# A norm gain folded into the weights' high/low split, a new order of the first tiles, and a shorter output norm in a hybrid block

## The reference

```python
hn = rms_norm(x, attn_norm)                  # x * rsqrt(mean(x^2) + eps) * gain
proj = hn @ w_in                             # one combined projection
qkv = silu(causal_depthwise_conv(proj[qkv columns], conv_w))
q = l2_normalize(q) * 128 ** -0.5            # 4 heads of 128; k likewise without the factor
o_a = gated_delta_rule(q, k, v, g, beta)     # chunks of 64 tokens, state carried over
o_a = rms_norm(o_a, gdn_out_norm) * silu(gate)
o_b = multiscale_pool(proj[pool columns]);  o_c = chunk-causal attention (MLA)
x = x + concat(o_a, o_b, o_c) @ w_out
x = x + SwiGLU(rms_norm(x, ffn_norm)) @ w_down
```

## Time and profile before

| | |
|---|---|
| Median of 3 runs | 1188.63 us (1188.12 to 1191.61) |
| The profiled execution | 1188.19 us, of which the span from first to last instruction is 1186.2 us |
| Instructions in the span | 16437 |
| Input projection, tiles 2 to 21 | 41 to 301 us |
| Delta rule and attention | about 300 to 475 us |
| Output projection and SwiGLU | from about 500 us to the end |

### The profile page before, as it was taken

The page is one execution under the profiler, slowest core; times in us unless marked ns, Lnnn a source line. Parts: engine busy times, 40 slices in busy tenths (PEclk is TensorE's granted clock), DMA queues, the critical chain, the costliest instruction groups (busy, mean ns, idle before and its releaser), DMA issues.

```text
span 1186.2 us, 16437 instructions
## 1 busy us (share of the span) xinstructions
PE 1176.0 (99%) x6049; PEld 974.6 (82%) x6049; DVE 812.8 (69%) x1246; ACT 445.4 (38%) x778; POOL 386.1 (33%) x351
## 2 busy tenths in 40 slices
PE   8999999999999999999999999999999999999998
PEld 7888878887788888888888888888888888888887
DVE  6548777997778764447765665656565687868686
ACT  5322222432333332345433333333333353535342
POOL 5001111440221221024456565665665346000000
PEclk9999999999999999999999999999999999999999
DMA  8411344683575210424246656554684369565544
GB/s 265 128 36 36 107 123 119 192 243 103 145 247 148 72 58 1 160 89 125 85 153 216 203 178 220 180 169 151 213 302 141 115 205 317 175 200 173 168 144 172
DMA packets 196980, 186.14 MB, mean 157 GB/s; under 512 B 23495, under 2 KB 152917, under 8 KB 196901
## 3 DMA queue, kind: packets, MB, share of 16 engines
q1 hardware_dynamic: 196750, 185.05, 49.7%
q10 hardware_dynamic: 150, 0.05, 0.0%
HBM read 126.75 MB, written 57.26 MB: 155 GB/s over the span
## 4 chain that ended last, share of the span: by engine, by line
PE 53%; ACT 0%; DVE 0%; issue 0%
PE ps L2629 35%; PE ps L2634 18%; ACT hT L1551 0%; PE ps L2566 0%; DVE x L2162 0%
## 5 line engine op out<-in xcount | busy, mean ns | idle before, releaser
L2629 PE MATMUL ps<-xop,wop_hi 128*128 128x512 f32 x1232 | 379.5, 389 | 0.0
L2629 PEld LDWEIGHTS ps<-xop,wop_hi 128*128 128x128 f32 x1232 | 231.0, 188 | 48.4 <-DVE wop_lo L2074 0.6
L2629 PE MATMUL ps<-xop,wop_lo 128*128 128x512 f32 x616 | 239.6, 389 | 0.0
L2634 PE MATMUL ps<-dop,wop_hi 128*128 128x512 f32 x440 | 136.0, 390 | 0.1
L2629 PEld LDWEIGHTS ps<-xop,wop_lo 128*128 128x128 f32 x616 | 115.6, 188 | 24.1
L2074 DVE TENSOR_TENSOR wop_lo<-w_sumS,wop_hi 128x512 fp32r<-128x512 f32 (+1 forms) x104 | 83.1, 802 | 67.1 <-ACT wop_hi L1521 67.1
L2074 DVE TENSOR_TENSOR wop_lo<-w_pair,wop_hi 128x512 fp32r<-128x512 f32 (+1 forms) x76 | 84.7, 1115 | 34.1 <-ACT wop_hi L1521 34.1
L2162 DVE TENSOR_TENSOR x<-x,ps 128x512 f32<-128x512 f32 x112 | 76.6, 684 | 45.5 <-PE ps L2634 45.2
L2213 PE MATMUL ps<-act_hi,w_hi 128*128 128x512 f32 x320 | 100.7, 396 | 0.2 <-DVE stage L1787 0.2
L2213 PE MATMUL ps<-act_lo,w_hi 128*128 128x512 f32 x320 | 98.8, 390 | 0.0
L2213 PE MATMUL ps<-act_hi,w_lo 128*128 128x512 f32 x320 | 98.6, 389 | 0.0
(11 more groups left out here) (364 smaller groups left out, 2157.3 us busy)
## 6 DMA issues: line engine op xcount, KB each, us to landing
w_pair<-in_w_gate_up SPq DMA_DIRECT2D x44, 512.0 KB, 5.3
hidden<-up SPq DMA_DIRECT2D x22, 512.0 KB, 2.9
wd_rows<-in_w_down SPq DMA_DIRECT2D x22, 512.0 KB, 5.2
raw<-in_w_in SPq DMA_DIRECT2D x21, 512.0 KB, 4.6
wd_raw<-down_sums SPq DMA_DIRECT2D x12, 768.0 KB, 7.1
down_sums<-wd_rows SPq DMA_DIRECT2D x33, 256.0 KB, 2.6
wd_raw<-in_w_down SPq DMA_DIRECT2D x9, 768.0 KB, 8.0
qkv_kept<-qkv_st SPq DMA_DIRECT2D x12, 512.0 KB, 5.4
```

What stands on the lines that cost most here:

```text
L2629: last = pe.matmul(ps[:, bank, :].rearrange("p (t n) -> p t n", n=P), w[:, k, :], a[:, k, :, :], start=(p in ("P1", "P2", "P7") and k == 0 ...
L2634: last = pe.matmul(ps[:, bank, :], w[:, k, :], a[:, k, :], start=(p in ("P1", "P2", "P7") and k == 0 and w is wop_hi[s] and a is hi), stop ...
```

## The change

It does five things.

- The gain attn_norm is no longer multiplied into the tokens. It comes in as 8 rows of 128, PE turns it into a column per block (in_gain), and the tokens are multiplied by rstd alone, by a tensor_scalar.
- The gain goes into the weights at the split. As it differs from block to block, split_hi and split_lo become 8 instructions over 128 columns each in place of one over 1024; each has in_gain[:, k] as its factor per partition. This holds for every tile from 1 to 21; the narrow tile is multiplied once.
- At the start: 14 and 8 warm-up matmuls in place of 5 and 4, no spreading of the gain row, token tile 3 turned before the narrow tile, the quarter of tile 1 after more of the narrow tile; ACT squares a token tile after act_hi of the one three before, not ahead of it; the splits of tiles 0 and 1 come one step later on ACT, and one and two steps later on DVE. SP's order of loads is the same as before, though the loop is written in another way.
- The output norm of the delta rule goes under one root: mean(o^2) * rq^2 + eps becomes mean(o^2) + 128 * eps * (ss + eps), whose inverse root is the whole factor. The root of the queries' square sums on POOL and four small DVE instructions in each chunk go.
- The first inverse step reads A's lower left 32x32 blocks directly (32 rows in place of 64) and no longer a masked copy B. POOL's m0 stage, its mask, and the wait on it go.

Left out of the diff: the constants and the mask tensor, and POOL_ORDER without its qk and m0 entries.

```diff
--- before.py
+++ after.py
@@ -282,9 +280,10 @@
...
     x_sq = prep[:, 0, :]
-    x_gain_row = prep[:, 2, :]
+    gain_rows = prep[0:KT, 2, 0:P]
     x_in = [sgT[:, j, :] for j in range(3)] + [prep[:, 1, :]] + [cT[:, j, :] for j in range(2)] + [x_six[:, :], pz[:, 0, :]]
-    C_CONV, C_FFN, C_QA, C_KVA, C_GDN, C_POOL, C_POS, C_QK = 0, 48, 56, 58, 59, 60, 62, 70
+    C_CONV, C_FFN, C_QA, C_KVA, C_GDN, C_POOL, C_POS, C_QK, C_IN = 0, 48, 56, 58, 59, 60, 62, 70, 72
+    in_gain = cols[:, C_IN:C_IN + KT]
 
...
@@ -352,9 +351,9 @@
...
 
-        mid_pe = Steps(sem("mid_pe"), ["gain0", "gain1", "cols", "decays", "log_row", "pool0", "pool1"])
+        mid_pe = Steps(sem("mid_pe"), ["in_gain", "cols", "decays", "log_row", "pool0", "pool1"])
         mid_act = Steps(sem("mid_act"), ["exp_abs", "exp_alog", "exp_b", "ln", "kr_sq", "kv_weights", "decays", "log_col", "log_row", "pool0", "pool1"])
-        mid_dve = Steps(sem("mid_dve"), ["positions", "abs", "kv_scaled", "one_plus", "g"])
+        mid_dve = Steps(sem("mid_dve"), ["in_gain", "small_scaled", "positions", "abs", "kv_scaled", "one_plus", "g"])
 
...
@@ -388,10 +387,10 @@
...
         ga = [Steps(sem(f"gdn_act{b}"), ["sq", "x1", "m1", "x2", "osq"], ahead=True) for b in range(2)]
-        gd = [Steps(sem(f"gdn_dve{b}"), ["et", "att", "ss", "kd", "vn", "rqs", "r2", "n1", "n2", "r0", "r", "o1",
-                                         "v", "s", "o", "osum", "oms0", "oms", "of", "on", "out"], ahead=True)
+        gd = [Steps(sem(f"gdn_dve{b}"), ["et", "att", "ss", "kd", "vn", "n1", "n2", "r0", "r", "o1",
+                                         "v", "s", "o", "osum", "oms", "on", "out"], ahead=True)
               for b in range(2)]
-        gg = [Steps(sem(f"gdn_pool{b}"), ["rq", "b0", "sd", "pow"], ahead=True) for b in range(2)]
+        gg = [Steps(sem(f"gdn_pool{b}"), ["sd", "pow"], ahead=True) for b in range(2)]
         GROUPS = (1, 0)
...
@@ -765,7 +764,8 @@
...
             load_in_tile(1, 1)
-            for t in range(RAW, TT):
+            load_x(RAW)
+            for t in range(RAW + 1, TT):
                 load_x(t)
...
@@ -1177,16 +1167,7 @@
...
                 for stage_name, b, i in order:
-                    if stage_name == "qk":
-                        sc = tok_sc[b]
-                        pool.wait_ge(gd[b].sem, gd[b].after("ss", i))
-                        pool.tensor_tensor(sc[:, 12:16], sc[:, 0:4], half_neg[:, 0:4], ALU.pow).then_inc(gg[b].sem, 1)
-                    elif stage_name == "m0":
-                        pool.wait_ge(a_loaded[b], i * 16 + 16)
-                        pool.wait_ge(gd[b].sem, gd[b].after("o", i - 1))
-                        pool.tensor_tensor(B_[b][:, :, :], A_[b][:, :, :], heads_of(masks[:, 0, :]),
-                                           ALU.mult).then_inc(gg[b].sem, 1)
-                    elif stage_name == "ks":
+                    if stage_name == "ks":
                         pool.wait_ge(gd[b].sem, gd[b].after("et", i))
...
@@ -1279,7 +1260,7 @@
...
 
-            act.dma_start(x_gain_row[0:1, :], attn_norm[:, :]).then_inc(prep_loaded, 16)
+            act.dma_start(gain_rows, attn_norm[0].rearrange("(k p) -> k p", p=P)).then_inc(prep_loaded, 16)
             act.wait_ge(consts_ready, 1)
...
@@ -1294,24 +1275,30 @@
...
 
-            AHEAD = 3
-            for t in range(AHEAD):
+            def high_weights(slot, rawslot):
+                for k in range(KT):
+                    op = act.activation(w_hi[slot][:, k, :], raw[rawslot][:, k, :], ACT.Copy, scale=in_gain[:, k:k + 1])
+                op.then_inc(hi_split, 1)
+
+            for t in range(3):
                 x_square(t)
             for t in range(TT):
-                if t + AHEAD < TT:
-                    x_square(t + AHEAD)
                 act.wait_ge(x_turned, t + 1)
                 act.activation(act_hi[:, :, tile_cols(t)], x_turned_view(t), ACT.Copy).then_inc(x_high, 1)
-                if t == 0:
-                    act.wait_ge(small_loaded, 2 * 16)
+                if t + 3 < TT:
+                    x_square(t + 3)
+                if t == 1:
+                    act.wait_ge(mid_dve.sem, mid_dve.after("small_scaled"))
                     act.activation(w_hi[0][:, :, 0:SMALL], small_raw, ACT.Copy).then_inc(hi_split, 1)
-                if t == 1:
+                if t == 2:
+                    act.wait_ge(mid_dve.sem, mid_dve.after("in_gain"))
                     act.wait_ge(x_loaded[1], loaded_count(1))
-                    act.activation(w_hi[1][:, :, :], raw[1][:, :, :], ACT.Copy).then_inc(hi_split, 1)
+                    high_weights(1, 1)
+
             def split_hi(m, slot, rawslot, rnd):
...
                 act.wait_ge(x_loaded[rawslot], rnd)
-                act.activation(w_hi[slot][:, :, :], raw[rawslot][:, :, :], ACT.Copy).then_inc(hi_split, 1)
+                high_weights(slot, rawslot)
 
...
@@ -1436,7 +1423,9 @@
...
                         gafter(gp[b], "x1")
-                        gsig(b, act.activation(X1[b], blocks_view(U[b]), ACT.Copy))
+                        for lower, upper in BASES:
+                            op = act.activation(X1[b][upper, :, :], blocks_view(U[b], upper), ACT.Copy)
+                        gsig(b, op)
                     elif stage_name == "m1":
...
@@ -1605,35 +1594,38 @@
...
                 dve.wait_ge(x_rstd, t + 1)
-                dve.scalar_tensor_tensor(x_in[t], x_in[t], rstd[:, t:t + 1], x_gain_row, ALU.mult, ALU.mult).then_inc(x_scaled, 1)
+                dve.tensor_scalar(x_in[t], x_in[t], rstd[:, t:t + 1], None, ALU.mult).then_inc(x_scaled, 1)
 
...
 
-            for h in range(HALVES):
-                half = slice(h * BANK, (h + 1) * BANK)
-                dve.wait_ge(mid_pe.sem, mid_pe.after(f"gain{h}"))
-                link(dve.tensor_copy(x_gain_row[:, half], ps[:, 6 + h, :]))
-                dve.wait_ge(x_rstd, 1)
-                op = dve.scalar_tensor_tensor(x_in[0][:, half], x_in[0][:, half], rstd[:, 0:1], x_gain_row[:, half],
-                                              ALU.mult, ALU.mult)
-            op.then_inc(x_scaled, 1)
+            def low_weights(slot, rawslot):
+                for k in range(KT):
+                    op = dve.scalar_tensor_tensor(w_lo[slot][:, k, :], raw[rawslot][:, k, :], in_gain[:, k:k + 1],
+                                                  w_hi[slot][:, k, :].bitcast(f32), ALU.mult, ALU.subtract)
+                op.then_inc(raw_used, 1)
+
+            dve.wait_ge(mid_pe.sem, mid_pe.after("in_gain"))
+            dve.tensor_copy(in_gain, ps[:, 7, 0:KT]).then_inc(mid_dve.sem, 1)
+            dve.wait_ge(mid_dve.sem, mid_dve.after("in_gain"))
             for t in range(TT):
-                if t > 0:
-                    x_scale(t)
+                x_scale(t)
                 if t >= 2:
...
                 if t == 2:
+                    dve.wait_ge(small_loaded, 2 * 16)
+                    dve.tensor_tensor(small_raw, small_raw, in_gain.unsqueeze(2).broadcast_to([P, KT, SMALL]),
+                                      ALU.mult).then_inc(mid_dve.sem, 1)
+                    dve.wait_ge(mid_dve.sem, mid_dve.after("small_scaled"))
+                if t == 3:
                     dve.wait_ge(hi_split, 1)
...
                                       ALU.subtract).then_inc(raw_used, 1)
-                if t == 3:
+                if t == 5:
                     dve.wait_ge(hi_split, 2)
-                    dve.tensor_tensor(w_lo[1][:, :, :], raw[1][:, :, :], w_hi[1][:, :, :].bitcast(f32),
-                                      ALU.subtract).then_inc(raw_used, 1)
-                if t == 5:
+                    low_weights(1, 1)
                     dve.wait_ge(rows_loaded, 7 * 16)
...
@@ -1644,8 +1636,7 @@
...
                 dve.wait_ge(hi_split, m + 1)
-                dve.tensor_tensor(w_lo[slot][:, :, :], raw[rawslot][:, :, :], w_hi[slot][:, :, :].bitcast(f32),
-                                  ALU.subtract).then_inc(raw_used, 1)
+                low_weights(slot, rawslot)
 
...
@@ -1948,17 +1939,13 @@
...
                         gafter(ga[b], "sq")
-                        own("r2", i - 1)
-                        gsig(dve.tensor_scalar(sc[:, 0:4], sc[:, 44:48], EPS, None, ALU.add))
+                        own("oms", i - 1)
+                        gsig(dve.tensor_scalar(sc[:, 36:40], sc[:, 44:48], EPS, EPS * GDN_DIM, ALU.add, ALU.mult))
                     elif stage_name == "turn":
...
                             k_len[:, chunk_at, :].rearrange("p a h -> p (a h)")), ALU.mult))
-                        gafter(gg[b], "rq")
-                        gsig(dve.tensor_scalar(sc[:, 12:16], sc[:, 12:16], float(GDN_DIM) ** -0.5, None, ALU.mult))
-                        own("rqs")
-                        gsig(dve.tensor_tensor(sc[:, 36:40], sc[:, 12:16], sc[:, 12:16], ALU.mult))
                     elif stage_name == "y1":
...
@@ -1993,14 +1980,10 @@
...
```

(44 more changed lines are left out.)

9 lines of the change are left out of this document (removed).

## The result

The changed kernel took 1224.41 us (median of 4 runs, 1222.2 to 1225.36) against 1188.72 us (4 runs of the kernel before): ratio 1.0291, 95% interval 1.0277 to 1.0305. It is slower by 35.7 us. The forecast was 1218 us with a range of 1203 to 1232.

The account below looks back on a forecast made before the run. PE was busy 99%, but in tiles 6 to 13 the loop through ACT and DVE was taken to be as long as PE's work. 29 + 1.7 + 1.5 - 2 = +30 us on 1188.19 gave 1218 us, range 1203 to 1232.

Parts of the forecast that it names:

- the largest term: Input projection, tiles 6 to 13: the split in eight pieces adds 2.5 us per pass, +20.8 us on PE in all.
- The loop through ACT and DVE: Tiles 6 to 13: last tap, silu, split_hi, split_lo, taps; its period of 13.88 us is as long as PE's 13.79.
- The price of a piece: 128-column pieces of the split: starts 0.31 us apart on ACT, 0.28 on DVE; eight add 1.5 and 1.0 us.
- The cheap rival: Splits: the factor costs nothing in a stream of like instructions, 1.25 us per pass, 1200 to 1205 us; chance 0.20.
- Tiles 14 to 17, +3.7: Input projection: ACT's part exposed once more (+1.5), DVE gets 4 x 1.0; PE 24.5 us late at product 19, +3.7 us.
- Tiles 19 and 20, +4.1: Both engines' splits count, DVE 29.0 us late; PE's third score maximum waits for the reduction, 28.6 late, +4.1 us.
- Start +1.5: First token tiles, warm-ups and tile 1's first quarter in the new order: net +1.5 us, bounds -1 and +4.
- tile 2 +1.7: Pieces of split_hi(2) and split_lo(2) end at 42.8 us, while product 2 started at 41.06: +1.7 us.
- Delta rule, -2: Delta rule: PE idles 1.4 us, 0.5 for the shortened chain; modelled ends may hide more: -2 us, bounds 0 and -4.
- The clock: Sign of failure, tiles 6 to 13: PE's clock falling in waits; held unlikely, as a 3.1 us start wait left it high.

## Why the prediction was right, and where its sum was off

The mechanism of the largest term was right, and the runs show it. The total came as near as it did partly by luck: two later terms were too large for what they described, and a collision with POOL that the sum didn't have took their place and more.

- *The loop through ACT and DVE bounds tiles 6 to 13, and pieces lengthen it.* Shown, by taking them out, by putting them alone into the kernel before, and by moving them out of the loop. 2.5 us a pass was forecast, 2.36 measured (16.24 - 13.88); 20.8 us for the stretch, 19.9 measured.
- *The price of a piece.* ACT 0.31 us apart forecast, 0.29 measured (2.44 us in all, forecast 2.6); DVE 0.28 forecast, 0.26 measured (2.20, forecast 2.3). Alone they cost 1.40 and 0.97 us a pass. The cheap rival, 1.25 us a pass, is out. What share of a piece is its factor stays open, since no run has pieces without one. By the Trainium skill's formulas ("VectorE: DVE Perf Modes", TRN2 errata) I had estimated 1.3 and 0.4 us: near for ACT, less than half of the truth for DVE. The measurement decides.
- *Tiles 14 to 17, +3.7.* This is the step that failed in size: 11.7 us. "DVE gets 4 x 1.0" took a piece's price as the same everywhere. In tiles 17 to 19 pieces met POOL's gtg products and took 5.1, 5.1 and 5.9 us, 2.9 to 3.7 more than alone. In the kernel before the whole split met them too, in tiles 16 and 17, but as one instruction it lost only 0.5 and 1.1 us (1.67 and 2.31 in place of 1.22). Holding POOL back brought the stretch to +1.6, below the forecast, so my own term without the collision was even too high. That 1.6 is half clock, but PE then started product 19 only 0.3 us behind DVE's last tap; without the fall it would have waited for the tap and lost about 1.4 (estimate).
- *Tiles 19 and 20, +4.1.* 1.7 us measured, and it isn't the wait that I described: PE has no wait there, and the 1.7 is the half clock from 296.7 us. DVE was 36.0 us late at the last tap of tile 17 and only 34.9 at the first reduction; the 0.81 us that it idled ahead of split_lo(20) is gone, so ACT's part didn't count. Without the fall, PE would have come to the third score maximum at 305.2, before the reduction's end at 305.7 (estimate), and lost some 0.5. Where the wait for the reduction does show, with POOL held back and with ACT's pieces alone, it is 0.4 and 0.9 us.
- *Start +1.5 and tile 2 +1.7.* split_hi(2) began 1.0 us later (38.87 against 37.87) and the pieces added 1.5: 2.5 in all. But the same code differs by 2 us here from run to run.
- *Delta rule, -2.* 0.2 to 0.7 us. What I had supposed hidden in PE's modelled ends wasn't there; the 0.5 us wait that the table of waits names was nearly all.
- *The clock.* I had argued that waits of 2.4 us leave it high. Wrong: it fell behind five of them. Inside the loop it cost nothing, since the wait that follows shrinks; where PE is the bound, one fall costs 1.6 to 1.9 us, and 1.7 of the 35.7 are such a fall.

Sum: 30 forecast, 1.0 + 1.5 + 19.9 + 11.7 + 1.7 - 0.7 = 35.1 measured; the last 0.9 us of the span lies behind PE's last matmul and I have no cause for it. Two small slips in the forecast: 1218.3 + 0.4 is 1218.7 and not 1218, and the DVE pieces' 2.3 - 1.22 is 1.1 and not 1.0 (0.97 measured).

## What to carry to other kernels

Before an operation is split up, find the loop that it stands in: eight instructions a tile cost 1.4 us a pass between ACT's silu and DVE's split, and nothing in the same tiles a few us further on, in ACT's own idle time. When a long instruction on DVE becomes many short ones, look at what POOL runs beside them: each of POOL's can hold up another of the short ones. And before a step is moved to an idle POOL, look at which DVE instructions will lie beside it, down to those of four columns.
